# A value projection tile ahead of the stick-breaking scores, and a weight transfer ahead of the second tile of x

## The reference

```python
for l in range(DEPTH):
    h = rms_norm(x, norm1_g[l])
    proj = h @ w_in[l]                         # 1024 -> 6 * 512
    da_q, da_k, da_v, sb_q, sb_k, sb_v = jnp.split(proj, SPLITS, axis=-1)
    # differential attention: two softmaxes for each of 4 heads, a = p0 - lam * p1, then a @ v
    o_da = diff_attention(q, k, v, lam)        # q, k: per-head RMSNorm and partial RoPE
    # stick-breaking attention, 8 heads of 64
    z = q @ k.T * scale                        # strict causal mask
    log_fail = where(strict, log_sigmoid(-z), 0)
    after = cumsum(log_fail, reverse=True) - log_fail
    a = where(strict, exp(log_sigmoid(z) + after), 0)
    o_sb = a @ v
    x = x + concat([o_da, o_sb]) @ w_out[l]
    x = x + hierarchical_moe(rms_norm(x, norm2_g[l]), ...)   # 32 experts, top 2 in the top group
```

## Time and profile before

| | before |
|---|---|
| median of 3 runs | 815.44 us (813.14 to 817.92) |
| the profiled execution, device time | 821.89 us |
| its span, first to last instruction | 820.0 us |
| mean granted clock of TensorE | 0.928 |
| PE busy | 685.2 us (84%) |
| DVE busy | 303.4 us (37%) |
| ACT busy | 127.6 us (16%) |
| bytes moved | 240.06 MB, mean 293 GB/s |
| longest stretch that DMA engines are nearly idle in layer 0 | 93 to 117 us, 24 GB/s |

### The profile page before, as it was taken

One profiled execution on the slowest core, in us unless ns is written; L12 is line 12 of the kernel. 1 busy time (PEld: TensorE's weight loads), 2 busy tenths in 40 slices (PEclk: granted clock), 3 DMA queues, 4 the chain that ended last, 5 costly groups with the idle time before them and its releaser, 6 DMA issues.

```text
span 820.0 us, 10368 instructions
## 1 busy us (share of the span) xinstructions
PE 685.2 (84%) x3684; PEld 343.6 (42%) x3685; DVE 303.4 (37%) x674; ACT 127.6 (16%) x318; POOL 9.0 (1%) x19
## 2 busy tenths in 40 slices
PE   8998999987886887586699989998787868885774
PEld 5444456564333243231244454646434333332321
DVE  0336732352442344232325364335332324332313
ACT  3114521200000000000031343211000000000000
POOL 0000000010000000000020000000000000000000
PEclk8998999988998999898899989998897989998987
DMA  8797128437998899999995240654199869999991
GB/s 295 244 400 277 42 103 352 178 43 272 422 422 329 346 405 422 422 422 415 392 364 223 103 154 1 253 234 180 44 413 419 357 256 367 418 422 422 422 400 56
DMA packets 49987, 240.06 MB, mean 293 GB/s; under 512 B 7648, under 2 KB 7936, under 8 KB 25376
## 3 DMA queue, kind: packets, MB, share of 16 engines
q1 hardware_dynamic: 49344, 238.61, 73.0%
q0 software_dynamic: 608, 0.99, 1.0%
HBM read 238.54 MB, written 1.05 MB: 292 GB/s over the span
## 4 chain that ended last, share of the span: by engine, by line
PE 59%; DMA 16%; issue 12%; DVE 5%; DVEq 2%; PEldq 2%; PEld 2%; ACT 1%; SPq 1%; ACTq 1%
PE bank L1065 19%; DMA wbuf<-in_w_down 10%; PE bank L1190 7%; PE bank L1212 7%; PE bank L1162 7%; PE bank L1229 5%; DMA wbuf<-in_w_up 5%; PE bank L1240 4%; PE bank L1122 1%; PE bank L1109 1%; PE bank L1085 1%; DMA wbuf<-in_w_in 1%; PE bank L1142 1%; PEld bank L1212 1%; PEldq L1231 1%
## 5 line engine op out<-in xcount | busy, mean ns | idle before, releaser
L1065 PE MATMUL bank<-wbuf,hTbuf 128*128 128x512 f32 x384 | 171.5, 603 | 1.9 <-DMA wbuf<-in_w_in 1.4
L1212 PE MATMUL bank<-wbuf,qkT 128*32 128x512 f32 x1024 | 113.2, 594 | 4.8 <-DMA wbuf<-in_w_up 3.6
L1065 PEld LDWEIGHTS bank<-wbuf,hTbuf 128*128 128x128 f32 x384 | 73.0, 193 | 91.1 <-issue 89.4
L1190 PE MATMUL bank<-qkT,xn 128*128 128x128 f32 x512 | 75.4, 316 | 40.0 <-issue 40.0
L1229 PE MATMUL bank<-wbuf,qkT 128*32 128x512 f32 x512 | 74.0, 703 | 35.1 <-DMA wbuf<-in_w_down 27.4
L1190 PEld LDWEIGHTS bank<-qkT,xn 128*128 128x128 f32 x512 | 72.4, 229 | 52.9 <-issue 52.9
L804 DVE TENSOR_TENSOR x_sb<-x_sb,bank 128x512 f32<-128x512 f32 x72 | 46.3, 684 | 76.9 <-PE bank L1240 76.9
L1212 PEld LDWEIGHTS bank<-wbuf,qkT 128*32 128x32 f32 x1024 | 31.6, 110 | 83.2 <-issue 74.6
L1162 PE MATMUL bank<-wbuf,hTbuf 128*128 128x512 f32 x128 | 56.0, 593 | 0.0
L1229 PEld LDWEIGHTS bank<-wbuf,qkT 128*32 128x32 f32 x512 | 15.8, 122 | 83.1 <-issue 54.3
L526 ACT ACTIVATE qkT<-bank 128x256 f32<-128x256 f32 x18 | 6.9, 384 | 192.9 <-PEq L1215 192.9
(11 more groups left out here) (204 smaller groups left out, 601.7 us busy)
## 6 DMA issues: line engine op xcount, KB each, us to landing
wbuf<-in_w_gate SPq DMA_DIRECT2D x64, 1024.0 KB, 13.0
wbuf<-in_w_up SPq DMA_DIRECT2D x64, 1024.0 KB, 16.2
wbuf<-in_w_down SPq DMA_DIRECT2D x64, 1024.0 KB, 11.5
wbuf<-in_w_in SPq DMA_DIRECT2D x24, 1024.0 KB, 14.6
wbuf<-in_w_out SPq DMA_DIRECT2D x8, 1024.0 KB, 6.3
x_sb<-in_x SPq DMA_DIRECT2D x2, 512.0 KB, 4.4
out<-x_sb SPq DMA_DIRECT2D x1, 1024.0 KB, 4.0
cst<-in_const SPq DMA_DIRECT2D x1, 548.0 KB, 13.1
```

The source lines that it names most:

```text
L1065: last = MM(ps[PROJ_BANK[i][t]][:, :], hT[:, k, t * P:(t + 1) * P], block_rows(i, k), start=(k == 0), stop=(k == KC - 1))
L1190: last = MM(ps[k // 4][:, (k % 4) * P:(k % 4 + 1) * P], xn[:, t, k * P:(k + 1) * P], sel[:, t, :], start=(t == 0), stop=(t == TT - 1))
L1212: MM(ps[bank][j * SLOTS:(j + 1) * SLOTS, :].rearrange("p (a f) -> p a f", a=2), src[:, k, j * SLOTS:(j + 1) * SLOTS], halves[:, gate:up + ...
```

## The change

Four edits. In the order of the tensor engine and of the scalar engine, in both layers, P(4,0) stands ahead of the transposes of the stick-breaking keys, P(5,0) takes the place that P(4,0) had, and P(4,1) the place that P(5,0) had; nothing is left in the place that P(4,1) had, ahead of `attend(l, 0)`. `transpose_qk(l, 3)` now stands ahead of `da_transpose(l, 0)` and `(l, 1)`. In layer 0 the transfer of the first half of block 0 stands ahead of that of x tile 1, and PE transposes x tile 1 in the middle of P(0,0), between its fourth and fifth matmul. ACT takes both norms ahead of its half of tile 1. `params(0)` is transferred after block 3, no longer after block 1.

```diff
             sp_.dma_start(g1T[:, :], gain1(0)).then_inc(g1_in[0], 16)
+            load_half(0, 0, 0)
             sp_.dma_start(x_sb[:, 1, :], x[0, P:2 * P, :]).then_inc(x_in[1], 16)
-            for i in range(IN_BLOCKS):
+            load_half(0, 0, 1)
+            for i in range(1, IN_BLOCKS):
                 load_block(0, i)
                 if i == 1:
                     sp_.dma_start(cst[:, C_GE:], const[:, C_GE:]).then_inc(const_in, 16)
                     for dst, src in gains(0):
                         sp_.dma_start(dst, src).then_inc(gains_in[0], 16)
+                if i == 3:
                     for dst, src in params(0):
                         sp_.dma_start(dst, src).then_inc(par_in[0], 16)
@@ scalar engine
-                for t in range(TT):
-                    hT_half(2 * l, t, g1T)
-                for t in range(TT):
-                    if l == 0:
+                if l == 0:
+                    hT_half(0, 0, g1T)
+                    for t in range(TT):
                         act.wait_ge(x_in[t], 16)
-                    else:
-                        act.wait_ge(x_done, l)
-                    norm(l, t)
+                        norm(0, t)
+                    hT_half(0, 1, g1T)
...
                 qkT_half(l, 2)
+                softmax_exp(l, 2)
+                proj_tile(l, 4, 0)
                 qkT_half(l, 3)
                 daT_copy(l, 0)
                 daT_copy(l, 1)
-                softmax_exp(l, 2)
                 softplus_ln(l, (4, 5))
                 softplus_ln(l, (0, 1))
-                proj_tile(l, 4, 0)
+                proj_tile(l, 5, 0)
                 daT_copy(l, 2)
                 softplus_ln(l, (2, 3))
                 break_exp(l, 4)
                 break_exp(l, 5)
-                proj_tile(l, 5, 0)
+                proj_tile(l, 4, 1)
                 for w in range(4):
                     break_exp(l, w)
-                proj_tile(l, 4, 1)
@@ tensor engine, proj_tile
                     if i == 0 and k == KC // 2:
+                        if l == 0 and t == 0:
+                            pe.wait_ge(x_in[1], 16)
+                            transpose_x(1)
                         pe.wait_ge(block0_rest_in, (l + 1) * 16)
@@ tensor engine, the layer
                 transpose_qk(l, 2)
-                pe.wait_ge(proj_out, l * 12 + 8)
+                proj_tile(l, 4, 0)
+                transpose_qk(l, 3)
                 da_transpose(l, 0)
                 da_transpose(l, 1)
-                transpose_qk(l, 3)
                 pe.wait_ge(qkT_d, l * 4 + 4)
                 pe.wait_ge(qkT_a, l * 4 + 4)
                 sb_scores(l, 4, 5)
                 sb_scores(l, 0, 1)
-                proj_tile(l, 4, 0)
+                proj_tile(l, 5, 0)
                 pe.wait_ge(daT_out, l * 3 + 1)
                 da_transpose(l, 2)
...
                 sb_scores(l, 2, 3)
-                proj_tile(l, 5, 0)
+                proj_tile(l, 4, 1)
                 for w in range(4):
                     cumulate(l, w)
-                proj_tile(l, 4, 1)
                 attend(l, 0)
                 proj_tile(l, 5, 1)
```

More of the change, by code:

```diff
@@ L564, in _ @@
                 act.wait_ge(g1_in[l], 16)
-                for t in range(TT):
-                    hT_half(2 * l, t, g1T)
-                for t in range(TT):
-                    if l == 0:
+                if l == 0:
+                    hT_half(0, 0, g1T)
+                    for t in range(TT):
                         act.wait_ge(x_in[t], 16)
-                    else:
-                        act.wait_ge(x_done, l)
-                    norm(l, t)
+                        norm(0, t)
+                    hT_half(0, 1, g1T)
+                else:
+                    for t in range(TT):
+                        hT_half(2 * l, t, g1T)
+                    act.wait_ge(x_done, l)
+                    for t in range(TT):
+                        norm(l, t)
                 act.wait_ge(lam_dot, l + 1)
@@ L1302, in _ @@
                     pe.wait_ge(x_done, l)
[L1303 to L1306, removed]
+                if l == 0:
+                    pe.wait_ge(x_in[0], 16)
+                transpose_x(0)
+                if l > 0:
+                    transpose_x(1)
                 proj(l, 0)
```

## The result

The changed kernel takes 807.12 us (median of 4 runs, 804.68 to 809.87), the kernel before 816.27 in the runs beside it (4 runs, 813.14 to 817.92): a ratio of 0.9893 with a 95% interval of 0.9848 to 0.9939. By the medians it is 9 to 13 us faster, by the two intervals together 5 to 15; the forecast was 11.15, and 804.3 us.

The account below looks back on a forecast made before the run. The prediction took PE's own work as the bound (59% of the chain's span, transfers 16%). Gains of 5.1 (layer 0), 5.55 (layer 1) and 0.5 (start) sum to 11.15 us: 815.44 to 804.3 us, range 800 to 809.5.

Parts of the forecast that it names:

- P(4,0) starts at 74.11: Layer 0, PE: the tile follows the queries' transposes at once, ends at 80.98 and covers the 2.11 us row-maximum wait.
- The gains of 5.1 and 5.55 us: Attention parts of layers 0 and 1: time won by the new tile order, up to the start of P(5,1).
- The two new waits: PE waits for ACT ahead of the scores of 2, 3 and inside attend(l, 0): 0.6 and 0.75 us.
- I take 0.6: Ahead of the scores of 2, 3: PE waits for ACT's copy, computed as 0.55 us and taken as 0.6.
- 0.75 us: Inside attend(0, 0): the second half waits for the last exp, ready at 109.45 with PE there at 108.7.
- the clock still falls: Rival: clock drops at the bunched transposes or new waits, up to 3.4 us a layer, giving 811.1 us; 5%.
- The cold stretch stays: Start: the clock fell at about 9.3 in PE's idle time and will fall again, that time being longer.
- Gain 0.5 us: Start: P(0,0) begins near 8.6, less 0.93 us for uncovered transposes; bounds a loss of 1.4 to a gain of 1.2.
- the start does not do what it says: Rival: block 0's half still lands at 10.0 and the transposes cost 0.93 us, giving 805.7 us; 8%.
- the transfers' rival: Transfers in the full expert part set the end anyway, so nearly nothing arrives: 815 us; 5%.
- all of it moves with that point: Expert part: the weight stream starts at a point set by the attention part, so gains count in full.
- The chain through DVE and ACT: Rival: from the scores to attend this chain, not PE, is the bound and starts 1.26 us later: 817.4 us; 4%.

Follow-up runs that it names:

- e1_order: The changed kernel with its start put back (transfers, params, norms and transposes as before), leaving only the new tile order: 806.51 us, ratio 0.9856 to before.
- e7_split: The changed kernel with the first matmul of P(4,1) ahead of the scores of 2, 3 and of P(5,1) between attend's halves: 806.95 us, ratio 0.9868.
- e4_filled: The kernel before, with 8 and 3 throwaway matmuls per layer in PE's waits ahead of the keys' transposes and the scores: 813.15 us, ratio 0.9951.
- e2_start: The kernel before with only the start edited (transfers, order of x tile 1, params later), tile order of before: 816.9 us, ratio 0.9997.
- e3_mid: The kernel before with x tile 1's transposes in the middle of P(0,0), but x tile 1 transferred ahead of block 0: 818.8 us, ratio 1.0006.
- e6_slope: The changed kernel with 24 throwaway matmuls ahead of attend(l, 0) in both layers: 812.39 us, ratio 0.9932 to before.
- e11: The new tile order with the start of before, plus 4 and 5 throwaway matmuls in PE's two waits at the start: 805.58 us, ratio 0.9834.
- e5: The changed kernel with 10 throwaway matmuls behind x tile 0's transposes, while PE waits for block 0's first half: 803.28 us, ratio 0.9836.
- e12: New tile order, start of before with 4 and 5 throwaway matmuls, and first matmuls of P(4,1) and P(5,1) moved into the new waits: 801.72 us, ratio 0.9792.
- e8: The changed kernel with 10 throwaway matmuls at the start and first matmuls of P(4,1) and P(5,1) moved into the new waits: 805.48 us, ratio 0.9857.
- e10: The changed kernel with 48 throwaway matmuls ahead of attend(l, 0) in both layers: 815.2 us, ratio 0.997 to before.

## Why the prediction was right

- **The stretch of the scores.** "P(4,0) starts at 74.11", right behind the queries' transposes, the row maximum under it, and from there the tile at full clock: all as in the profile after. The forecast played the order forward and had P(5,1) 38.02 us behind the queries' transposes (111.2 less 73.18); it is 38.00. The gains of 5.1 and 5.55 us were 5.13 and 5.59, and e1_order shows that they belong to the order of the tiles alone. The prediction named two waits and the clock in the stretch of 10.30 us; a third wait, 0.52 us (0.84 in layer 1), stands there too. Playing the order forward from 74.11 took it in without naming it, and it is where the 0.33 by which it counted layer 1 higher comes from.
- **The two new waits were taken too long, and other terms made up for it.** "I take 0.6" for the wait of the scores of 2, 3: it is 0.28, and 0.35 in layer 1. ACT's copy began at 92.33 and ended at 92.90, 21.31 us behind the queries' transposes, as forecast (94.50 less 73.18 is 21.32). But PE reached it later than assumed: `cumulate` ended near 92.67, 21.08 behind, where 20.9 was forecast, and the handoff was 0.05 where 0.15 was taken. The row behind this is P(5,0) with `da_transpose(l, 2)`, 7.52 us from start to start (83.19 to 90.71) where the forecast took 7.31. It had taken 0.1 off the 7.41 of before for P(4,0)'s slow first passes; that tile showed 7.13 us there, the same as P(5,0). "0.75 us" inside `attend(l, 0)` is 0.55 in both layers. Together the waits lack 0.52 us, and PE's rows and handoffs around them took as much longer, so the sum holds. That it holds to 0.03 us is luck; e7_split shows that the waits are real, since covering both gives 0.83.
- **The clock.** The sixteen transposes in a row, at 79.39, left it at 1.00, and so did the new waits where they stand: none of the ten profiles with this order has a row below 1.00 in its attention parts. The rival "the clock still falls" is out. The Trainium skill ("TensorE: Matmul & The Clock Gate", Part 4) says that transposes don't count as a busy PE in the way matmuls do. No row of this case shows an effect of it: the sixteen took 1.84 us (79.39 to 81.23) at a granted clock of 1.00. e4_filled shows the other half, that the slow scores came from the idle time and not from the instructions: 22 passes of filling made the keys' transposes and the scores run at 1.06 and 2.03 us, in the order of before.
- **How much the clock cost before** was read from one execution. The forecast took 10.30 and 10.63 us for the stretch up to P(4,0); e2_start and e3_mid, whose attention is that of before, have 9.24 and 9.22 in layer 0 and 10.37 and 9.67 in layer 1. By those profiles the two layers give 8.6 to 9.8 us, not 10.65; by the medians of e1_order, 10.6 (interval 8.5 to 15.0). A term read off one execution was right here to within 2 us, not to within its decimals.
- **The start.** "The cold stretch stays" and "Gain 0.5 us". P(0,0) began at 8.90, not at 8.6: it won 1.16 us where 1.46 were forecast. The transposes cost 0.89, near the 0.93 of the forecast. What was wrong is the cold stretch (the time at 1.2 GHz), which was 3.4 us long and not 6.8, and so this execution gained 1.59, more than the upper bound of 1.2. But e1_order has none with the start of before, and e2_start a long one with the new start; one profile does not tell its length. Nor does one tell when P(0,0) begins: with the new transfers it was 8.90, 9.04, 9.17, 9.22, 9.32, 9.37, 9.37 and 10.44 (e6_slope), with the old ones 10.06, 10.12, 10.39, 10.52, 10.62 and 11.32 (e4_filled). Median against median the start is worth nothing that can be measured (0.9997), and 0.1 to 0.4 us in the profiles when the clock is held (e11 against e5, e12 against e8). For this term the rival "the start does not do what it says" came about as near as the forecast, a matter of 0.5 us of 11; its mechanism, a half block that lands at 10.0 all the same, is seen in e6_slope alone.
- **Does it reach the end?** The forecast counted the gains in full. From P(5,1) of layer 0 to the first expert matmuls it is 63.36 us where it was 63.37, and both spans and medians moved by about the sum. So the transfers' rival is out for this change. The general sentence, "all of it moves with that point", is too strong: of 19.8 us added in e10 only 10.7 arrived in the median, and in the two profiles the expert parts are 13.4 us shorter, by shorter pauses and by a higher granted clock. That the change was not touched by this is seen in its profile (231.94 and 240.97 against 232.20 and 241.20). That other kernels would be, no row of before showed. The stretches from P(5,1) to the experts vary too: 60.7 to 63.5 us over all profiles.
- **How near the total is.** Attention parts and start together gave 12.3 us in the pair of profiles where 11.15 were forecast, and the spans moved by 14.0; the medians moved by 9.2 and 12.8 us in the two comparisons. That 11.15 lies between these is as much as the measurement can say.
- **The chain through DVE and ACT** was not the bound. It starts 1.24 us later (82.47 less 71.59, against 82.82 less 73.18), and PE's wait for it in `attend` is only the 0.55.

## What to carry to other kernels

Where an engine stands idle for a vector reduction and the clock falls in that time, the price is the wait and then the slow work behind it: here 3.4 to 3.7 us of waits and 2.65 us of slow work a layer in the profile of before, and in others as little as 1.6 us of the latter. Move a piece of independent work of the wait's size into it, and play the order forward row by row on each engine; that gave the gain within 0.1 us here, with the new waits foreseen by their place and sizes that were off by 0.5 us and made up elsewhere. A transfer moved ahead of another has to win more than the work costs that it takes out of cover (here 1.16 against 0.89 us), so price the uncovered work first. And before a gain of 1 us is read from one pair of profiles, look at what the untouched parts do between executions: here the runs of the kernel before alone go from 808.6 to 822.1 us.

## What the runs showed that was not expected

- The same start can run with or without a fall of the clock. With waits of 1.09 and 1.39 us (before) it was at 1.2 GHz for 6.8 us; with 1.21 and 1.47 (e1_order) it never fell. In the changed kernel, with one wait of 2.43, it was 3.4 us, and in e6_slope, with one of 4.16, 6.8.
- PE's pauses ahead of the gather, in which it waits for nothing visible, add up to 32.3 us in e10 and 41.0 in e5, and change when instructions are added or taken away far ahead of them. Kernels with a busy start (e5, e8, e11, e12) all have 235.1 to 235.4 us in layer 0's expert part, the changed kernel 230.4 to 231.9. In layer 1 it is the other way round, 235.6 to 237.9 against 240.6 to 241.0, so that the sums of both are alike (470.7 to 473.2 and 471.1 to 472.9). Read one layer's expert part alone, and a cost appears that the whole kernel doesn't have.
- A matmul for nothing can be worth its time: eleven of them a layer, 2.8 us of PE's work put into waits of before, made the kernel 3.9 us faster (interval 1.5 to 6.6).
